# Forgetting attention in a fused three-layer block: both transposes of a pair together and two steps later, gate pieces behind the value products

## The reference, cut to what matters

```
u = x @ w_in + b_in
mq, mk, mv, mo, mi, mf, fq, fk, fv, ff = split_sizes(u, ...)
h_ml = sigmoid(mo) * head_norm(mlstm_chunkwise(...))
def block(i):                                   # 128 queries
    logits = q_i @ k^T * scale + F[q] - F[k]    # keys 0 .. 128*(i+1)
    logits = where(kpos <= qpos, logits, -inf)
    p = softmax(logits)
    return p @ v
y = concatenate([h_ml, h_fx]) @ w_out
x = layer_norm(ALPHA * x + y)
```

## Time and profile before

| | |
|---|---|
| median of 3 runs | 2119.8 us (2119.24 to 2120.02) |
| time of the profiled execution | 2119.8 us, span of its trace 2118.0 us |
| PE | 2096.6 us busy, 99% of the span, 10324 matmul records |
| DVE, ACT, POOL | 1267.0, 920.6 and 137.0 us busy |
| chain that ended last | PE 87%, DVE 7%, ACT 4% |
| mean granted TensorE clock | 0.999 |

### The profile page before, as it was taken

How to read it: one execution, slowest core, us unless ns; L and a number is a source line. 1 busy time by engine, 2 the same in 40 slices (tenths; PEclk the granted TensorE clock), 3 DMA queues, 4 the chain that set the end, 5 groups by cost and what they waited for, 6 DMA issues and landing times.

```text
span 2118.0 us, 26124 instructions
## 1 busy us (share of the span) xinstructions
PE 2096.6 (99%) x10324; PEld 1709.9 (81%) x10324; DVE 1267.0 (60%) x1945; ACT 920.6 (43%) x1549; POOL 137.0 (6%) x186
## 2 busy tenths in 40 slices
PE   9999999999999999999999999999999999999998
PEld 7866688888888758888888878887788878888887
DVE  7446575555436778655553748665678856555534
ACT  4235553333425466333342643264455745333421
POOL 0000040000000112200000000000132500000000
PEclk9999999999999999999999999999999999999999
DMA  5312123333232423332333322212432023322331
GB/s 207 99 56 84 62 96 93 99 100 114 95 100 91 129 90 120 100 99 91 119 100 96 123 81 81 98 31 80 149 118 82 22 80 120 99 91 98 120 97 72
DMA packets 58553, 205.60 MB, mean 97 GB/s; under 512 B 6360, under 2 KB 9520, under 8 KB 57408
## 3 DMA queue, kind: packets, MB, share of 16 engines
q1 hardware_dynamic: 58432, 203.93, 29.6%
HBM read 199.62 MB, written 4.28 MB: 96 GB/s over the span
## 4 chain that ended last, share of the span: by engine, by line
PE 87%; DVE 7%; ACT 4%; issue 1%; DMA 1%; SPq 0%; POOL 0%; DVEq 0%; ACTq 0%
PE bank L526 26%; PE bank L528 26%; PE bank L527 26%; PE bank L1093 2%; DVE wlo L2064 1%; PE bank L814 1%; PE bank L795 1%; ACT arena L1389 1%; ACT whi L1284 1%; DMA ring<-stream 1%; DVE small L2090 1%; DVE arena L2211 1%; DVE arena L2643 0%; DVE xs L2085 0%; PE bank L886 0%
## 5 line engine op out<-in xcount | busy, mean ns | idle before, releaser
L526 PE MATMUL bank<-xs,whi 128*128 128x512 f32 (+2 forms) x1992 | 768.3, 386 | 4.8 <-DVE xs L2085 2.9
L528 PE MATMUL bank<-xs,wlo 128*128 128x512 f32 (+2 forms) x1992 | 749.4, 376 | 0.0
L527 PE MATMUL bank<-xs,whi 128*128 128x512 f32 (+2 forms) x1992 | 749.2, 376 | 0.0
L2064 DVE TENSOR_TENSOR wlo<-ring,whi 128x1024 fp32r<-128x1024 f32 x333 | 416.8, 1253 | 291.0 <-ACT whi L1284 290.7
L1284 ACT ACTIVATE whi<-ring 128x1024 fp32r<-128x1024 f32 x333 | 350.2, 1053 | 256.6 <-DMA ring<-stream 256.3
L526 PEld LDWEIGHTS bank<-xs,whi 128*128 128x128 f32 x1992 | 375.0, 188 | 89.7 <-issue 14.0
L528 PEld LDWEIGHTS bank<-xs,wlo 128*128 128x128 f32 x1992 | 374.8, 188 | 68.9
L527 PEld LDWEIGHTS bank<-xs,whi 128*128 128x128 f32 x1992 | 375.2, 188 | 68.2 <-issue 3.1
L526 PE MATMUL bank<-whi,xs 128*128 128x512 f32 (+1 forms) x776 | 300.5, 387 | 1.5 <-issue 1.0
L528 PE MATMUL bank<-whi,xs 128*128 128x512 f32 (+1 forms) x776 | 298.7, 385 | 0.0
L527 PE MATMUL bank<-wlo,xs 128*128 128x512 f32 (+1 forms) x776 | 298.7, 385 | 0.0
(11 more groups left out here) (379 smaller groups left out, 1756.0 us busy)
## 6 DMA issues: line engine op xcount, KB each, us to landing
ring<-stream SPq DMA_DIRECT2D x333, 512.0 KB, 3.5
arena<-gains SPq DMA_DIRECT2D x5, 1024.0 KB, 5.8
arena<-gate_rows SPq DMA_DIRECT2D x16, 256.0 KB, 3.8
arena<-xt SPq DMA_DIRECT2D x4, 512.0 KB, 5.9
arena<-xn SPq DMA_DIRECT2D x1, 2048.0 KB, 7.9
arena<-step_rows SPq DMA_DIRECT2D x4, 512.0 KB, 4.1
kept<-arena SPq DMA_DIRECT2D x1, 2048.0 KB, 7.2
arena<-factor_rows SPq DMA_DIRECT2D x8, 256.0 KB, 5.0
```

The source lines that it names most:

```text
L526: nc.tensor.matmul(out, ah, bh, start=first, stop=False)
L527: nc.tensor.matmul(out, ah, bl, start=False, stop=False)
L528: return nc.tensor.matmul(out, al, bh, start=False, stop=last)
L2064: V.tensor_tensor(wlo[:, v % SLOTS, :], ring[:, v % SLOTS, :], whi[:, v % SLOTS, :], ALU.subtract).then_inc(wlo_done, 1)
```

## The change

PE issues no transposes at odd slots. At even slots from 6 on it issues those of both steps of a pair, T(n-6) and T(n-5), where before it issued T(n-4) in slot n and T(n-3) in slot n+1. ACT's pt moves from slot k+4 to slot k+6, one per slot as before. The pieces of a gate unit now stand at slots 1, 3 and 5 (3, 3 and 2 pieces) of groups of eight slots, that is only at odd slots, behind V. The gate's Exp on ACT moves with them from slots 7, 14, 21, 28 to 6, 14, 22, 30, and its later operations likewise. The number of matmuls, activations and vector operations stays the same. Nothing changes on POOL and SP.

```
-        MO_FIRST, MO_STEP = 2, 7
-        mo_pieces = {MO_FIRST + MO_STEP * j + x: [(("mo", j), k) for k in ks] for j in range(4) for x, ks in enumerate(((0, 1), (2, 3), (4,), (5, 6), (7,)))}
+        MO_FIRST, MO_STEP = 1, 8
+        mo_pieces = {MO_FIRST + MO_STEP * j + 2 * x: [(("mo", j), k) for k in ks] for j in range(4) for x, ks in enumerate(((0, 1, 2), (3, 4, 5), (6, 7)))}
...
                 for n in range(N + 8):
-                    if 4 <= n < N + 4:
-                        k, st = n - 4, fox_steps[n - 4]
-                        b = 5 + k % 2
+                    for k in (n - 6, n - 5) if n % 2 == 0 and 6 <= n < N + 6 else ():
+                        st, b = fox_steps[k], 5 + k % 2
                         claim(b)
                         pe.wait_ge(vector_out, vector_at.find("fox", "p", k))
...
-                    if 4 <= n < N + 4:
-                        k, st = n - 4, fox_steps[n - 4]
+                    if 6 <= n < N + 6:
+                        k, st = n - 6, fox_steps[n - 6]
                         act.wait_ge(tensor_out, tensor_at.find("fox", "t", k))
```

## The result

The changed kernel takes 2125.59 us (median of 10 runs, 2123.95 to 2127.28), the one before 2119.57 beside it (10 runs, 2119.0 to 2120.02): ratio 1.0029, 95% interval 1.0022 to 1.0037, 6.0 us slower. Forecast were 2124.7 us, +4.9. What stands out beside the median is the spread: 3.3 us, where before it is 1.0 in this set. (In the later, larger sets of 21 to 33 executions the kernel before spreads over 1.3 to 2.6 us.)

A forecast was written before the change was run, and what follows sets the result against it. PE was taken to bound the attention, busy 75.2 of 77.6 us. New waits 8.6, less 3.2 for old waits and 0.4 for switches, gave +5.0, taken as +4.9 on 2119.8: 2124.7 us, 8-in-10 range 2120.5 to 2127.8.

The forecast's parts named there:

- slot 8: Second half of the four transposes behind L(6,7) waits for pt(1), behind exp(6) and the gate's Exp: 2.6 us lost.
- slot 10: Transposes T(5) wait for the copy pt(3), behind exp(8), a rounding and the gate's Ln and Exp: 0.7 us lost.
- T(11): Transposes at slot 16 wait for pt(9), behind exp(14) and the gate's Exp: 0.9 us lost.
- V(8,9): Value products behind slot 16's logits wait for the copy o(0), which stands behind exp(15): 1.1 us lost.
- T(27): Transposes in slots 31 to 33 wait behind exp(30), the gate's Exp of slot 30 and a rounding: 1.0 us.
- the term of -3.2: PE's five waits in the attention before the change, 2.3 us idle plus 0.17 each, taken out of the sum.
- the 0.4 of the sum: Eight fewer pieces directly behind logits on PE, each switch taken as 0.05 us: 0.4 us less.
- the reading by which the switches would be worth nothing: Only changes of tiling mode on PE cost, their number is equal in both orders: 0 in place of -0.4 us.
- rival D: Granted clock falls to 1.2 GHz in the longer waits, notably slot 8, adding 2 to 4 us: 2128; chance 0.03.
- A: Half the new waits at slots 16 and 24 are hidden, and 0.5 us at slot 8: about 2122 us; chance 0.14.
- B: Faster: old waits go and none replace them, if exp(6) starts by 184.3: 2116.9 us; chance 0.07.
- C: The loop closes at every pair: some six further pairs of transposes lose 0.5 us each, 2128 us; chance 0.10.

The follow-up runs named there:

- the run with filler: Changed kernel plus ten 128x512 matmuls whose results nothing reads, four and six at slot 8's transposes; 2125.59 us, ratio 1.0027.
- filler_all: Changed kernel plus 29 matmuls whose results nothing reads, in eight places where PE waits; 2123.98 us, ratio 1.0022.
- both_copies: Changed kernel with ACT copying both transposed steps of a pair at the even slot, ahead of its exp; 2122.01 us, ratio 1.0012.
- transposes_only: Changed kernel with the gate's pieces and Exp put back as before, so only transposes and their copies moved; 2123.74 us, ratio 1.0021.

## Why the prediction came out right, and where it did not

**The waits.** Right in place, and nearly in size. Lost time by starts, predicted and found in the profile after, in us: slot 8, 2.6 and 2.65 (from 186.09 to 187.15, and from 187.37 to 188.96); slot 10, 0.7 and 0.73 (in the run with filler, where the clock did not hide it); T(11) 0.9 and 1.04; V(8,9) 1.1 and 1.06; T(17) 0.2 and 0.3; T(19) 0.9 and 0.88; V(16,17) 0.2 and 0.1; T(21) 0.7 and 0.8; T(27) 1.0 and 1.06; the first part of out0 0.3 and 0.36. In all 8.6 and 9.0. The net of +4.9 is the stretch of filler_all, +4.9, and near its median, +4.6.

That the net fits to 0.1 us is partly luck. The waits found are 0.4 more than the forecast's. On the other side, the kernel before loses more than the term of -3.2: redone by starts its five waits cost 3.1, as forecast, but four delays too short for a row in the idle column (0.15 at 179.65, 0.10 at 188.03, 0.07 at 206.97, 0.16 at 220.47) add 0.5, and the sum has no term for them.

**Within the waits, one detail was wrong.** At slot 8 the text lets T(2) go at 185.7 and charges everything to T(3). In fact T(2) waited too, 0.90 us in the idle column, because pt(0) had moved behind exp(5). The sum was right since pt(1) sets its end either way. T(27) looks like a second such place, since its row names the scaled weights of DVE (L2240). But its own weights, p(27), were scaled six microseconds earlier, at 240.56 us (the last L2240 of 384 wide). What it waited for is pt(25), the copy that empties its bank, as forecast:

```profile
246.53 0.55 PE L847 MATMUL bank<-con,arena 128*128 128x128 f32 x3 [0.84 <-DVE arena L2240]
...
246.23 0.29 DVE L2240 TENSOR_SCALAR arena<-arena,small 128x128 f32<-128x128 f32 x1
...
245.88 0.59 ACT L1445 ACTIVATE arena<-bank 128x512 f32<-128x512 f32 x1
```

The copy ends at 246.47; the scaling that ends at the same moment, at 246.52, is that of step 30. The releaser that a row names is inferred from the signal that came last.

**The switches.** Logits directly to V, the one step that stood nowhere in the trace of before, costs 0.15 us from start to start after a bf16 matmul of 128 (197.23 to 197.38 in the profile after):

```profile
197.23 0.22 PE L834 MATMUL bank<-mqb,idb 128*128 128x128 bf16 x1
197.38 0.66 PE L861 MATMUL bank<-arena 128*64 128x128 f32 x8
```

Such a matmul itself takes 0.06 (two follow each other at 209.98 and 210.04), so the switch is 0.09, the value taken. Whether the eight switches saved are worth the 0.4 of the sum was not measured alone. By difference something like it is left: +4.9 of the stretch at full clock, less 9.0 of waits that came, plus 3.6 of waits and delays that went, is -0.5. This is an estimate from many starts rounded to 0.01 us; it speaks against the reading by which the switches would be worth nothing, but does not rule it out.

**The term that was missing.** The forecast had the clock at 1.00 and kept its fall as rival D, with 3 in 100 and "in the longer waits". The profile, of the slowest execution, shows it; that it happens in most is inferred from the times and from the mean clock, which is 0.998 in eight of the ten executions and at that level in only three of the 84 of the kernel before listed beside the later runs. The step that failed is that the sum has no term for the clock: the trace of before has only short holes there, and it says nothing of what 2.9 us with 0.2 us of work in it would do. The price given for a fall (2 to 4 us on top) was near: 2.1 us at slot 8, 1.4 at slot 17, some 1.4 to 1.6 in the median. Had that been in the sum, about 2126 would have been the forecast.

**The rivals.** A (half hidden) falls: the waits at slots 16 and 24 came in full. B (faster) falls as the text said: exp(6) started at 187.38, not 184.3. C (a wait at every pair) falls: slots 12, 14, 18, 20 and 28 have no idle row. D is half right, as said above; it was no alternative to the forecast but a consequence of it, and should have been priced as one.

## What to carry to other kernels

When two engines pass a buffer to and fro, count the slots between where one asks for it and where the other gives it back, and name what stands between on the giver's list; putting two requests together takes a slot away unless the answers are put together too. Here the same order of PE was 6.0 us slower than before with the copies one per slot, and about 1.5 us faster, in two sets, with both copies ahead of the exp and the group's copy a slot earlier. And a wait on TensorE may cost more than its length: look at the spread of the executions and at the granted clock behind the hole, and try matmuls whose results nothing reads. Before you put a spread down to your holes, look at the clock of the whole program: here it also fell at the head, which the change does not touch.

## What was not expected of the hardware

The granted clock fell to the lower level behind holes that are short and not even empty: at slot 8 behind two idles of 0.90 and 1.37 us with two transposes in between, at slots 16 and 17 behind 0.83 and 1.00 us with two transposes and a logits pair in between. The same holes at slots 16 and 17 left it at 1.00 in the profile of the changed kernel (0.82 and 0.99 us), so it is not the hole alone that decides; what else does is open. In the kernel before, whose single idles in this stretch reach 1.0 us, no fall was seen in its profile. Nor does the longest single idle decide: behind 1.92 us ahead of V(8,9) in both_copies the clock stayed at 1.00, longer than any of the idles in the stretch behind which it fell. At the head of the program it fell behind 2.06 and 2.28 us (transposes_only and both_copies).
